# Two transformer blocks on one core: order and banks at the borders of an attention stage changed

## The chip, the cores and the metric

One core of a Trainium2 chip runs the whole program, one launch, everything in fp32. The metric is device time in microseconds (us). A core has a matmul engine (PE, with its weight loads shown apart as PEld), a vector engine (DVE), a scalar engine (ACT), GpSimd (POOL) and a queue engine (SP). Each takes its instructions in the order in which the program lists them and waits on semaphores. PE writes its results into PSUM, eight banks of 128 partitions by 512 fp32 values.

## The reference

256 latent and 256 context tokens of width 1024 run through two layers of a first block, then the latent tokens through two layers of a second. Cut to what matters for the change:

```
first block, each layer:
  mq = rms_norm(rms_norm(c_q, g_qa) @ w_uq)        8 heads of 96: 64 plain, 32 rotated by position
  mk, mv = from rms_norm(c_kv, g_kva) @ w_ukv       mk = rms_norm([k_nope, k_rope], g_mk)
  y_mla  = softmax(mq mk^T / sqrt(96)) mv
  y_na   = softmax over a neighbourhood plus the context keys, with a bias
  x     += gate * merge(sigmoid(g1) * (y_mla @ w_mla_o) + sigmoid(g2) * (y_na @ w_na_o)) @ w_out
  x     += gate * squared_relu(h2 @ w_ff1) @ w_ff2
second block, each layer:
  y = [retention, state space, stick breaking, softmax over a memory], each gated by silu
  x += rms_norm(y @ w_out_2)
```

Layer 0 of the first block computes all 512 tokens, layer 1 needs queries of the 256 latent ones alone; its tiles are half as wide (256 columns).

## The kernel before

Every engine has one program, written out by hand in the order of its work (PE from line 546, ACT from 1314, DVE from 1878). Signals are counted: `signal` lets an instruction raise a semaphore, `event` gives the value on which another engine waits.

*Products.* A product that needs full precision is made of three in a faster format: activation and weight are each split into a high and a low part, and `split_product` (L576 to L580) multiplies high by high, low by high and high by low. The high part of a weight chunk is written by ACT (`split_weights`, L1426 and L1428), the low part by DVE (L1954 and L1957); `split_half` (L1442, L1967) does it in halves between tiles of the attention. The raw chunks come by DMA from SP, each when its slot is free.

*Banks.* `next_bank(key, until=, among=)` calls `take`, which gives the next bank of a ring and lets PE wait until the last user of that bank has signalled its `until`. Each set of banks `among` has a turn counter of its own; calls without `among` go round all eight. The sets in use are the five `TURN_BANKS` for scores and transposes of an attention, bank 5 for its value products, banks 6 and 7 (`GATE_BANKS`) for the gate tiles that fill it, and six `LATE_BANKS` in the second block.

*The way into the attention* (both layers). PE projects keys and plain values: for i from 0 to 9 (L861) a key tile every second step, from step 2 on the sum of squares of head i - 2 (`head_sum`, L659), up to step 7 a value tile. DVE copies the key tile out, ACT squares it, PE sums the squares with ones, ACT takes -0.5 ln and exp (`rms`, L1320 and L1322), DVE scales the key (L2293, L2295). Then come six query tiles (L892, 18 products each): tiles 0 and 3 hold the rotated parts of four heads, the others two heads each. After tiles 1 and 4 PE rotates (`turn_quad`, L665), after tiles 2, 3 and 5 it sums squares (`query_sum`, L889), after tiles 1, 4 and 5 it makes a tile of the latent values (L877). DVE lifts tile 0 or 3 out with its gain (`gain_quad`, L2320), ACT squares it (L1613), DVE applies sine and cosine (L2328 to L2330), adds squares (L2301) and scales the heads (`scale_query`, L2310, L2314); the tiles of two heads stay in their banks until the second head is scaled (`roped`).

*The attention* (`softmax_attention`, L696). Scores run three tiles ahead of transposes: PE score (L925), DVE maximum (L1924), ACT exp (L1397), DVE reciprocal and product (L1928, L1930), PE transpose (L730), ACT copy (L1391), PE value product (L933), DVE copy (L2354). The last two heads' queries are scaled by DVE between the first maxima. From tile 34 (layer 0) or 18 (layer 1) on, PE fills in the eight g1 gate tiles, whose exp ACT takes (`gate_exp1`, L1637).

*The way out.* ACT splits the attention's output (L1647), with the exp of the last g1 tile between its fourth and fifth piece, DVE makes the low parts (L2377). PE runs for n = 0 to 7 the tiles g2, mo, no (24, 12 and 12 products); all three of one n share a weight chunk. In layer 1 DVE makes the low part of the chunk of n = 0 (L1957) after the last copy of the attention.

*The second block* ends each layer with a small attention over a memory (`per` = 2). Behind its last score PE does the first half of output tile 0 (`first_half`, L1214), and then both halves of all eight output tiles (L1206 to L1208), copied out by DVE (L2756).

Of the kernel before, what the change touches and what calls it, by code (L numbers as in the profile page):

```python
# [35 lines left out]
ALU = mybir.AluOpType  # L36
# [3 lines left out]
P = 128  # L40
D, L, T, TC = 1024, 2, 256, 256
KT = D // P
# [14 lines left out]
LINE = 128  # L57
TURN_BANKS, VALUE_BANKS, GATE_BANKS = (0, 1, 2, 3, 4), (5,), (6, 7)
LATE_BANKS = (0, 1, 2, 3, 4, 5)
FILL_FROM, FILL_STEPS = (34, 18), (4, 2)  # L60
GATES = [4, 5, 6, 7, 0, 1, 2, 3] + list(range(8, 16))
ADA = 24
# [201 lines left out]
def program(nc, dram, numbers):  # L264
# [3 lines left out]
    with ctx:  # L268
# [218 lines left out]
        def quad(g):  # L487

            return krope[:, 1 + g, :]
# [57 lines left out]
        def _(pe):  # L547
            used = {"chunk": -1, "open": set()}

            def next_bank(*key, until, among=None):  # L550

                return take(pe, "bank", key, until, among)
# [106 lines left out]
                mm = pe.matmul(ps[0:QK, 0:w], ones[0:QK, 0:QK], s[0:QK, 0:w], start=True, stop=True)  # L659
                full(mm, "ss", (name, i), l)  # L660

            def rotate(key, rows, src, until):

                ps = next_bank(*key, until=until)
                mm = pe.matmul(ps[rows, 0:T], c("rot")[rows, rows], src, start=True, stop=True)  # L665
                full(mm, *key)

# [132 lines left out]
            for l in range(L):  # L800
# [57 lines left out]
                project_heads("nk", 0)  # L858
                pe.wait_ge(*event("kr_gain", l))
                rotate(("krot", l), slice(NOPE, QK), krope[NOPE:QK, 2, TC:TT], ("krot_sin", l))  # L860
                for i in range(NH + 2):  # L861
                    if i < NH and i % 2 == 0:
                        ps = next_bank("mk", l, i // 2, until=("copied", "mk", l, i + 1))
                        mm = linear(ps[:, :], weights("uk", l, i // 2), lambda k: ckv[:, k, :], ("normed", "ckv", l))
                        full(mm, "mk", l, i // 2)
                    if i > 1:
                        head_sum("mk", i - 2, l, TT)

                    if i < NH:
                        nv_tile(l, i // 4, i % 4)  # L870

                def latent_values(t):

                    w = weights("uv", l)
                    ps = next_bank("mv", l, 0, t, until=("v_copied", "mv", l, 0, t))
                    for k in range(2):
                        mm = pe.matmul(ps[:, :], ckv[:, k, P * t:P * t + P], w[:, k, :], start=k == 0, stop=k == 1)  # L877
                    full(mm, "mv", l, 0, t)

                def turn_quad(g):  # L880

                    pe.wait_ge(*event("q_gain", l, g))
                    rotate(("qrot", l, g), slice(0, P), quad(g)[:, TC:TT], ("q_roped", l, g))

                def query_sum(i):

                    ps = next_bank("ss", ("mq", i), l, until=("rs_log", ("mq", i), l))
                    pe.wait_ge(*event("q_added", l, i))
                    mm = pe.matmul(ps[:, 0:cw], pair, given("sq", (("mq", i), l, 0))[:, 0:cw], start=True, stop=True)  # L889
                    full(mm, "ss", ("mq", i), l)  # L890

                for i in range(6):  # L892
                    g, part_of = divmod(i, 3)
                    by = ("q_added", l, 2 * g + 1) if part_of == 0 else ("roped", "mq", l, 4 * g + 2 * part_of - 1)
                    ps = next_bank("mq", l, i, until=by)
                    w = split_weights(("uq", l, i))
                    for k in range(6):
                        if i == 0:
                            pe.wait_ge(*event("cq_lo", l, k))
                        mm = split_product(ps[:, 0:cw], w, k, cq_hi[k][:, t0:TT], cq_lo[:, k, t0:TT], 6)  # L900
                    full(mm, "mq", l, i)
                    if part_of == 1:
                        turn_quad(g)
                    if i in (2, 3, 5):
                        query_sum((0, 0, 0, 1, 0, 2)[i])
                    if i in VALUES_AT:
                        latent_values(VALUES_AT.index(i))
# [123 lines left out]
            for lw in range(L):  # L1031
# [181 lines left out]

                def first_half():  # L1214

                    output_half(next_bank("out2", l, 0, until=("out_copied", l, 0)), 0, 0)

                softmax_attention([(("memory", l), u, 2, mem_score, mem_value) for u in range(8)], 2, mem_gate, first_half)

# [95 lines left out]
        def _(act):  # L1315
# [135 lines left out]
            for l in range(L):  # L1451
# [129 lines left out]
                    projected_keys(lambda: head_rms("nq", 3, t0))  # L1581
                    rms("ckv", l, KVL, P, TT, ("normed", "ckv", l, 1))
                projected_heads("nk", 0)
                for i in range(NH + 2):
                    if i in (0, 2, 3):
                        split_weights(("nv", l, i // 2, i != 2), 1)
                    if i == 0:
                        high_cq(5)
                    if 5 < i < NH:
                        split_weights(("uq", l, i - 6), 1)  # L1590
                    if i < NH:
                        act.wait_ge(*event("copied", "mk", l, i))
                        square(("mk", i), l, 0, 1, mk[0:NOPE, i, :], slice(0, NOPE), kr=i < 4)
                    if i > 1:
                        rms(("mk", i - 2), l, QK, QK, TT, ("k_ready", l, i - 2))
                    if i < NH:
                        j, t = divmod(i, 4)
                        copy_values("nv", l, j, t, nv[:, t, 256 * j:256 * j + 256], ("nv", l, j, t))
# [6 lines left out]
                for i in range(6):  # L1605
                    g, part_of = divmod(i, 3)
                    if i < 4:
                        split_weights(("uq", l, i + 2), 1)
                    act.wait_ge(*(event("psum_full", "mq", l, i) if part_of else event("q_gain", l, g)))
                    ps = bank(("mq", l, i))[:, 0:cw]  # L1610
                    for a in range(2 if part_of == 0 else 0):
                        v = take(act, "sq", ("rope", 2 * g + a, l), ("q_added", l, 2 * g + a))
                        act.activation(v[:, 0:cw], ps, ACT.Square, scale=c("half")[:, a:a + 1]).then_inc(*signal("rope_squared", l, 2 * g + a))  # L1613
                    if part_of:
                        square(("mq", 2 * g + part_of - 1), l, 0, 1, ps)
                    if i in (2, 3, 5):
                        query_rms((0, 0, 0, 1, 0, 2)[i])
                    if i in VALUES_AT:
                        latent_values(VALUES_AT.index(i))
# [19 lines left out]
                softmax([((g[0], l), u, P * g[6]) for g in groups(l) for u in range(2 * NH)], 4, split_gate, ("roped", "mq", l, NH - 1))  # L1639
                for n in range(-(-(16 * len(groups(l)) - FILL_FROM[l]) // FILL_STEPS[l]) - 1, KT - 1):  # L1640
                    gate_exp1(n)
                for k in range(KT):

                    if k == 4:
                        gate_exp1(KT - 1)
                    act.wait_ge(*event("y_copied", ("na", l), NH // 2 - 1))
                    act.activation(b_parts[:, 0, k, t0:TT], y_heads(k)[:, t0:TT], ACT.Copy).then_inc(*signal("b_hi", "y", l, k))  # L1647

# [230 lines left out]
        def _(dve):  # L1879
# [29 lines left out]
                dve.wait_ge(*event(before, *key))  # L1909
                dve.tensor_scalar(e, e, 1.0, 1e19, ALU.add, ALU.min).then_inc(*signal(name, *key))  # L1910

            def softmax(tiles, per, y_out, between=None):

                for i in range(len(tiles) + AHEAD + 3):
                    if i < len(tiles):
# [9 lines left out]
                    if 1 <= i <= len(tiles):  # L1925
                        g, v, w = tiles[i - 1]
                        dve.wait_ge(*event("exp", g, v))
                        then(dve.reciprocal(stat[:, v % 4, 2:3], stat[:, v % 4, 1:2]))  # L1928
                        e = given("prob", (g, v))[:, 0:w]
                        dve.tensor_scalar(e, e, stat[:, v % 4, 2:3], None, ALU.mult).then_inc(*signal("probs", g, v))  # L1930
                    j = i - AHEAD - 3
                    if per == 2 and j >= 0 and j % 2 == 0:
                        y_out(tiles[j][0], tiles[j][1] // 2)
# [127 lines left out]
            for l in range(L):  # L2061
# [213 lines left out]
                then(dve.tensor_tensor(kr, kr, c("cos")[NOPE:QK, :], ALU.mult))  # L2275
                dve.wait_ge(*event("krot_sin", l))
                then(dve.tensor_tensor(kr, kr, e, ALU.add))
                for i in range(NH + 2):
                    if i in (0, 2, 3):
                        split_weights(("nv", l, i // 2, i != 2), 1)  # L2280
                    if i == 0:
# [5 lines left out]
                        dve.wait_ge(*event("psum_full", "mk", l, i // 2))  # L2287
                        dve.tensor_copy(mk[0:NOPE, i, :], bank(("mk", l, i // 2))[r, :]).then_inc(*signal("copied", "mk", l, i))
                    if i > 1:
                        v = i - 2  # L2290
                        dve.wait_ge(*event("rs", ("mk", v), l))
                        r = given("rs", (("mk", v), l))
                        dve.scalar_tensor_tensor(mk[0:NOPE, v, :], mk[0:NOPE, v, :], p("g_mla_k", l)[0:NOPE, :],  # L2293
                                                 r[0:NOPE, :], ALU.mult, ALU.mult)
                        dve.tensor_tensor(mk[NOPE:QK, v, :], krope[NOPE:QK, 2, :], r[NOPE:QK, :], ALU.mult).then_inc(*signal("k_ready", l, v))  # L2295
                def add_rope(i):

                    v = given("sq", (("mq", i), l, 0))[:, 0:cw]
# [33 lines left out]
                for i in range(6):  # L2332
# [2 lines left out]
                        split_weights(("uq", l, i + 2), 1)  # L2335
                    if part_of == 0:
                        gain_quad(g)
                        if g:
                            scale_query(2)
                            scale_query(3)  # L2340
                    else:
# [27 lines left out]
                    for j, a in split_turn(l, i - 1):  # L2369
                        split_half(j, a)  # L2370

                softmax([((g[0], l), u, P * g[6]) for g in groups(l) for u in range(2 * NH)], 4, y_out, with_tile)
                if l:
                    split_weights(("g2", l, 0), 1)
                for k in range(KT):
                    dve.wait_ge(*event("b_hi", "y", l, k))
                    ins = dve.tensor_tensor(b_parts[:, 1, k, t0:TT], y_heads(k)[:, t0:TT],  # L2377
# [525 lines left out]
```

## Time and profile before

| | us |
|---|---|
| median of three runs | 1981.7 (1977.56 to 1983.45) |
| the profiled execution's own time | 1978.23 |
| its span in the trace | 1976.3 |
| PE busy | 1876.7 (95%) |
| DVE busy | 1358.1 (69%) |
| ACT busy | 913.2 (46%) |

The span is what the trace covers; 1.9 us of the execution lie around it. A busy share is a mean over stages. In a row of the timeline the bracket at the end tells how long the engine had been idle before the instruction and whose instruction ended the wait. PE instructions overlap a little, and their ends are modelled, so starts are the safer reading. The ways into the attention lie at 185 to 242 us (layer 0) and 984 to 1020 us (layer 1), the ways out at 366 to 380 and 1094 to 1106 us, the ends of the two memory attentions at 1609 to 1628 and 1906 to 1923 us.

### The profile page before, as it was taken

The numbers are of one execution on the slowest core, as the hardware profiler recorded it, in microseconds if no ns is written. First come the engines' busy times: TensorE is split into PE (matmuls) and PEld (weight loads), VectorE is DVE, ScalarE is ACT, GpSimd is POOL, SyncE is SP. The second block draws the span as 40 slices with busy tenths as digits, with TensorE's granted clock in tenths as the row PEclk, the third lists the DMA queues.
The fourth block names the chain that finished last, engine by engine and source line by source line (L and its number), as shares of the span: only waits on it lengthen the run. The fifth ranks groups of instructions, "written<-read, shape, count | busy, mean of one in ns | idle before, by whom it ended". The sixth has DMA issues, their size and how long they took to land.

```text
span 1976.3 us, 29270 instructions
## 1 busy us (share of the span) xinstructions
PE 1876.7 (95%) x11406; PEld 1590.3 (80%) x11406; DVE 1358.1 (69%) x2421; ACT 913.2 (46%) x1603; POOL 27.8 (1%) x56
## 2 busy tenths in 40 slices
PE   7999999999999999999999989999999989999997
PEld 3777556688888888887756889999999879999886
DVE  6666675688788887765577566665767755767764
ACT  3345565543423231354565654444444643544552
POOL 0000000000000000000000000000000000000000
PEclk9999999999999999999999999999999999999998
DMA  7332201255354545323132454444454325554322
GB/s 290 126 107 68 120 27 60 97 163 183 103 220 176 209 182 202 143 85 101 53 145 68 146 189 169 171 173 157 163 162 138 96 97 171 162 160 141 106 86 97
DMA packets 55896, 272.21 MB, mean 138 GB/s; under 512 B 6352, under 2 KB 7504, under 8 KB 38608
## 3 DMA queue, kind: packets, MB, share of 16 engines
q1 hardware_dynamic: 48272, 225.40, 33.1%
q0 software_dynamic: 7488, 44.94, 6.5%
q8 instruction: 92, 1.51, 0.3%
q14 instruction: 44, 0.36, 0.1%
HBM read 269.27 MB, written 1.05 MB: 137 GB/s over the span
## 4 chain that ended last, share of the span: by engine, by line
PE 71%; DVE 13%; ACT 9%; issue 5%; DMA 1%; SPq 0%; ACTq 0%; DVEq 0%
PE bank L578 18%; PE bank L580 17%; PE bank L579 17%; ACT w_parts L1428 3%; PE bank L925 2%; DVE small_lo L1954 2%; PE bank L933 2%; PE bank L730 2%; PE bank L614 2%; DMA wide<-in_ada 1%; PE bank L1206 1%; PE bank L1208 1%; PE bank L1207 1%; PE bank L625 1%; PE bank L1022 1%
## 5 line engine op out<-in xcount | busy, mean ns | idle before, releaser
L578 PE MATMUL bank<-h_hi,small_hi 128*128 128x256 f32 (+3 forms) x992 | 312.1, 315 | 12.3 <-DVE small_lo L1954 6.2
L579 PE MATMUL bank<-h_lo,small_hi 128*128 128x256 f32 (+3 forms) x992 | 301.8, 304 | 0.0
L580 PE MATMUL bank<-h_hi,small_lo 128*128 128x256 f32 (+3 forms) x992 | 301.7, 304 | 0.0
L1954 DVE TENSOR_TENSOR small_lo<-ring,small_hi 128x1024 fp32r<-128x1024 f32 (+1 forms) x192 | 226.4, 1192 | 107.4 <-ACT small_hi L1426 105.9
L579 PE MATMUL bank<-h_parts,w_parts 128*128 128x256 f32 (+1 forms) x784 | 262.8, 335 | 0.0
L1957 DVE TENSOR_TENSOR w_parts<-ring,w_parts 128x2048 fp32r<-128x2048 f32 x87 | 199.3, 2291 | 91.9 <-ACT w_parts L1428 91.9
L1428 ACT ACTIVATE w_parts<-ring 128x2048 fp32r<-128x2048 f32 x86 | 164.0, 1907 | 176.1 <-PE bank L580 176.1
L578 PE MATMUL bank<-b_parts,w_parts 128*128 128x256 f32 (+1 forms) x656 | 218.8, 334 | 1.5 <-DVE w_parts L1957 1.1
L580 PE MATMUL bank<-b_parts,w_parts 128*128 128x256 f32 (+1 forms) x656 | 217.9, 332 | 0.0
L579 PE MATMUL bank<-b_parts,w_parts 128*128 128x256 f32 (+1 forms) x656 | 217.8, 332 | 0.0
L578 PEld LDWEIGHTS bank<-h_hi,small_hi 128*128 128x128 f32 (+2 forms) x992 | 187.8, 189 | 26.9 <-issue 13.9
L579 PEld LDWEIGHTS bank<-h_lo,small_hi 128*128 128x128 f32 (+2 forms) x992 | 187.8, 189 | 10.9 <-issue 2.2
L1426 ACT ACTIVATE small_hi<-ring 128x1024 fp32r<-128x1024 f32 (+1 forms) x192 | 192.8, 1023 | 6.3 <-DMA ring<-in_w 6.1
L580 PEld LDWEIGHTS bank<-h_hi,small_lo 128*128 128x128 f32 (+2 forms) x992 | 187.6, 189 | 8.8
L578 PE MATMUL bank<-h_parts,w_parts 128*128 128x256 f32 (+1 forms) x528 | 178.4, 338 | 9.8 <-DVE w_parts L1957 4.2
L580 PE MATMUL bank<-h_parts,w_parts 128*128 128x256 f32 (+1 forms) x528 | 176.0, 333 | 0.0
L579 PEld LDWEIGHTS bank<-h_parts,w_parts 128*128 128x128 f32 x784 | 150.2, 192 | 13.5
L578 PEld LDWEIGHTS bank<-b_parts,w_parts 128*128 128x128 f32 x656 | 124.5, 190 | 15.1 <-issue 3.1
L580 PEld LDWEIGHTS bank<-b_parts,w_parts 128*128 128x128 f32 x656 | 124.6, 190 | 12.0
L579 PEld LDWEIGHTS bank<-b_parts,w_parts 128*128 128x128 f32 x656 | 124.6, 190 | 11.9
L578 PEld LDWEIGHTS bank<-h_parts,w_parts 128*128 128x128 f32 x528 | 101.2, 192 | 21.9 <-issue 9.3
L2010 DVE SCALAR_TENSOR_TENSOR prob<-lowrank,c_rows 128x1024 f32<-128x1024 f32 x96 | 113.3, 1217 | 0.0
(300 smaller groups left out, 3759.0 us busy)
## 6 DMA issues: line engine op xcount, KB each, us to landing
ring<-in_w SPq DMA_DIRECT2D x204, 512.0 KB, 3.5
ring<-in_w SPq DMA_DIRECT2D x96, 1024.0 KB, 4.8
lowrank<-in_rows POOLq DMA_DIRECT2D x24, 1024.0 KB, 5.1
prob<-in_rows POOLq DMA_DIRECT2D x24, 512.0 KB, 3.8
wide<-in_ada SPq DMA_DIRECT2D x8, 1024.0 KB, 9.9
ring<-in_w SPq DMA_DIRECT2D x14, 384.0 KB, 3.1
lowrank<-in_bias POOLq DMA_DIRECT2D x2, 2048.0 KB, 11.2
x<-in_x SPq DMA_DIRECT2D x2, 1024.0 KB, 9.9
```

Source lines behind the costliest of these rows:

```text
L578: pe.matmul(ps, w[0][:, k, :], hi, start=k == 0, stop=False)
L579: pe.matmul(ps, w[0][:, k, :], lo, start=False, stop=False)
L580: return pe.matmul(ps, w[1][:, k, :], hi, start=False, stop=k == nk - 1)
L614: mm = pe.matmul(out, w[:, k, :], src(k), start=first and k == 0, stop=last and k == nk - 1)
L730: mm = pe.transpose(ps[:, P * k:P * k + P], given("prob", (g, u))[:, P * k:P * k + P], ident)
L925: return pe.matmul(ps[:, 0:P * nk], qs[r, a, q:q + P], ks[r, a, 0:P * nk], start=True, stop=True)
L933: mm = pe.matmul(ps[VD * a:VD * a + VD, 0:T], vs[:, k, v:v + VD], turned[:, a, k, :], start=k == 0, stop=k == nk - 1)
L1426: act.activation(small_hi[:, pair, 0:size], small[:, slot, 0:size], ACT.Copy).then_inc(*signal("w_hi", i))
L1428: act.activation(w_parts[pair][:, 0, 0:size], ring[:, slot, 0:size], ACT.Copy).then_inc(*signal("w_hi", i))
L1954: dve.tensor_tensor(small_lo[:, slot, 0:size], small[:, slot, 0:size], small_hi[:, pair, 0:size].bitcast(F32), ALU.subtract).then_inc(*sig ...
L1957: dve.tensor_tensor(w_parts[pair][:, 1, 0:size], ring[:, slot, 0:size], w_parts[pair][:, 0, 0:size].bitcast(F32), ALU.subtract).then_inc(* ...
L2010: ins = dve.scalar_tensor_tensor((product1 if l else product if b < 40 else product2)[:, s, :], w, 1.0, c_rows[:, s, :], ALU.mult, ALU.mul ...
```

## The change

- The square sum of the last key head moves from before query tile 0 to after it on PE; its logarithm and exp (ACT) and its scaling (DVE) move behind the work on query tile 0.
- Query tiles 1 to 5 take banks 0, 3, 5, 6, 7; rotations and square sums of queries take turns in banks 1 and 4; latent value tiles take bank 2, the last of them bank 5. All of these took turns in all eight before.
- The exp of the last g1 tile moves ahead of the splitting of the attention's output.
- In layer 1 the low part of chunk n = 0 moves ahead of the last copies of the attention's output.
- The first half of output tile 0 takes a bank of `GATE_BANKS`.

```diff
+QUERY_BANKS, LATENT_BANKS, QUERY_TILES = (1, 4), (2,), (None, (0,), (3,), (5,), (6,), (7,))
 # PE
-            def rotate(key, rows, src, until):
+            def rotate(key, rows, src, until, among=None):
-                ps = next_bank(*key, until=until)
+                ps = next_bank(*key, until=until, among=among)
...
-                for i in range(NH + 2):
+                for i in range(NH + 1):
...
-                    ps = next_bank("mv", l, 0, t, until=("v_copied", "mv", l, 0, t))
+                    ps = next_bank("mv", l, 0, t, until=("v_copied", "mv", l, 0, t), among=VALUE_BANKS if t == 3 else LATENT_BANKS)
-                    rotate(("qrot", l, g), slice(0, P), quad(g)[:, TC:TT], ("q_roped", l, g))
+                    rotate(("qrot", l, g), slice(0, P), quad(g)[:, TC:TT], ("q_roped", l, g), QUERY_BANKS)
-                    ps = next_bank("ss", ("mq", i), l, until=("rs_log", ("mq", i), l))
+                    ps = next_bank("ss", ("mq", i), l, until=("rs_log", ("mq", i), l), among=QUERY_BANKS)
-                    ps = next_bank("mq", l, i, until=by)
+                    ps = next_bank("mq", l, i, until=by, among=QUERY_TILES[i])
                     full(mm, "mq", l, i)
+                    if i == 0:
+                        head_sum("mk", NH - 1, l, TT)
...
-                    output_half(next_bank("out2", l, 0, until=("out_copied", l, 0)), 0, 0)
+                    output_half(next_bank("out2", l, 0, until=("out_copied", l, 0), among=GATE_BANKS), 0, 0)
 # ACT
-                for i in range(NH + 2):
+                for i in range(NH + 1):
...
+                    if i == 0:
+                        key_rms(NH - 1)
                     if i in (2, 3, 5):
                         query_rms((0, 0, 0, 1, 0, 2)[i])
...
+                gate_exp1(KT - 1)
                 for k in range(KT):
-                    if k == 4:
-                        gate_exp1(KT - 1)
                     act.wait_ge(*event("y_copied", ("na", l), NH // 2 - 1))
 # DVE
+                    if beyond and i == len(tiles):
+                        beyond()
                     j = i - AHEAD - 3
...
-                for i in range(NH + 2):
+                for i in range(NH + 1):
...
                         gain_quad(g)
-                        if g:
+                        if g == 0:
+                            scale_key(NH - 1)
+                        else:
                             scale_query(2)
                             scale_query(3)
...
-                softmax([((g[0], l), u, P * g[6]) for g in groups(l) for u in range(2 * NH)], 4, y_out, with_tile)
-                if l:
-                    split_weights(("g2", l, 0), 1)
+                softmax([((g[0], l), u, P * g[6]) for g in groups(l) for u in range(2 * NH)], 4, y_out, with_tile,
+                        (lambda: split_weights(("g2", l, 0), 1)) if l else None)
```

`key_rms(i)` is the old `rms(("mk", i), ...)` and `scale_key(v)` the old pair of DVE instructions, each as a function.

## Rows read from the trace of the kernel before

**Rows 1.** Windows: stretch, us, busy PE, PEld, DVE, ACT, POOL, PEclk, DMA
```profile
374.00:520.00 146.00, 143.90 (x705) 122.11 (x704) 115.12 (x186) 65.53 (x92) 8.47 (x16) 0.99 0.43 144
520.00:700.00 180.00, 177.33 (x786) 146.88 (x786) 150.27 (x221) 54.21 (x53) 10.57 (x20) 0.99 0.54 194
```
**Rows 2.** Waits of PE, whole span: us in total, times, longest
```profile
PE bank L578 <- DVE w_parts L1957: 10.6, 13, 2.8
```
**Rows 3.** Timeline of PE, layer 0, last key sum and query tile 1: start, us
```profile
189.08 1.14 PE L659 MATMUL bank<-sq,con 96*96 96x512 f32 x1 [2.34 <-ACT sq L1334]
...
195.66 0.39 PE L578 MATMUL bank<-cq_hi,small_hi 128*128 128x512 f32 x1
```
**Rows 4.** Windows behind three waits of PE
```profile
189.10:192.15 3.05, 3.05 (x6) 1.68 (x6) 1.87 (x3) 2.99 (x6) 0.00 (x0) 0.50 0.06 24
...
373.70:376.40 2.70, 2.70 (x6) 2.16 (x7) 2.64 (x5) 2.70 (x5) 0.00 (x0) 0.50 0.00 0
...
1101.05:1103.90 2.85, 2.85 (x24) 2.85 (x25) 2.85 (x9) 2.33 (x3) 0.00 (x0) 1.00 0.66 201
```
**Rows 5.** Timeline of PE, layer 0, scores 2 and 3 and transpose 4
```profile
232.82 3.41 PE L925 MATMUL bank<-wide 96*128 96x512 f32 x4 [3.57 <-DVE wide L2314]
...
241.78 0.63 PE L730 MATMUL bank<-con,prob 128*128 128x128 f32 x4
```
**Rows 6.** Timeline of DVE, layer 0, maximum of score 2
```profile
234.56 0.69 DVE L1924 TENSOR_REDUCE stat<-bank 128x1 f32<-128x512 f32 x1 [1.79 <-PE bank L925]
```
**Rows 7.** Timeline of ACT, layer 0, exp of score 5
```profile
240.85 0.69 ACT L1397 ACTIVATE prob<-bank,stat 128x512 f32<-128x512 f32 x1
```
**Rows 8.** Timeline of PE, layer 0, last value product and first g2 tile
```profile
368.52 1.95 PE L933 MATMUL bank<-probT,wide 128*64 128x256 f32 x16 [0.73 <-issue]
373.69 0.80 PE L578 MATMUL bank<-h_hi,w_parts 128*128 128x512 f32 x1 [3.22 <-ACT wide L1637]
```
**Rows 9.** Timeline of PE, layer 1, key sum 6, rotation 0, query sum 0
```profile
984.77 1.02 PE L659 MATMUL bank<-sq,con 96*96 96x512 f32 x2
...
993.61 0.70 PE L665 MATMUL bank<-prob,con 128*128 128x256 f32 x2 [1.73 <-DVE prob L2320]
...
998.02 0.60 PE L889 MATMUL bank<-sq,con 128*128 128x256 f32 x2
```
**Rows 10.** Timeline of DVE, layer 1, scaling of key 7 and gain of tile 0
```profile
990.61 0.75 DVE L2293 SCALAR_TENSOR_TENSOR wide<-wide,par,rs 64x512 f32<-64x512 f32 x1
...
993.07 0.48 DVE L2320 TENSOR_SCALAR prob<-bank,gq 128x256 f32<-128x256 f32 x1
```
**Rows 11.** Timeline of ACT, layer 1, logarithm for key 7, squares of tile 0
```profile
989.01 0.67 ACT L1320 ACTIVATE rs<-bank,con 96x512 f32<-96x512 f32 x1
...
993.59 0.84 ACT L1613 ACTIVATE sq<-bank,con 128x256 f32<-128x256 f32 x2 [2.52 <-DVE prob L2320]
```
**Rows 12.** Timeline of PE, layer 1, first g2 tile
```profile
1101.05 0.36 PE L578 MATMUL bank<-h_hi,w_parts 128*128 128x256 f32 x1 [2.81 <-DVE w_parts L1957]
```
**Rows 13.** Timeline of ACT, layer 1, high parts of chunks 2 and 3
```profile
1107.56 1.90 ACT L1428 ACTIVATE w_parts<-ring 128x2048 fp32r<-128x2048 f32 x1
...
1114.09 1.90 ACT L1428 ACTIVATE w_parts<-ring 128x2048 fp32r<-128x2048 f32 x1
```
**Rows 14.** Timeline of DVE, layer 1, low part of chunk 1
```profile
1103.51 2.29 DVE L1957 TENSOR_TENSOR w_parts<-ring,w_parts 128x2048 fp32r<-128x2048 f32 x1
```
**Rows 15.** Timeline of DVE, second block, layer 0, first stick-breaking logits
```profile
1567.16 0.56 DVE L2662 TENSOR_SCALAR probT<-bank 128x384 f32<-128x384 f32 x1 [0.48 <-PE bank L1038]
```
**Rows 16.** Timeline of PE, second block, start of first half output tile, both layers
```profile
1615.23 0.39 PE L1206 MATMUL bank<-y_hi,small_hi 128*128 128x256 f32 x1 [1.62 <-DVE wide L2734]
...
1910.27 0.47 PE L1206 MATMUL bank<-y_hi,small_hi 128*128 128x256 f32 x1
```
**Rows 17.** Timeline of PE, second block, layer 1, start of output tile 1
```profile
1920.41 0.36 PE L1206 MATMUL bank<-y_hi,small_hi 128*128 128x256 f32 x1 [0.41 <-DVE small_lo L1954]
```
**Rows 18.** Timeline of DVE, second block, layer 1, copy of output tile 0
```profile
1921.31 0.42 DVE L2756 COPY probT<-bank 128x256 f32<-128x256 f32 x1
```

More of the change, by code:

```diff
@@ L1583, in _, with key_rms @@
                 projected_heads("nk", 0)
-                for i in range(NH + 2):
+                def key_rms(i):
+                    rms(("mk", i), l, QK, QK, TT, ("k_ready", l, i))
+                for i in range(NH + 1):
                     if i in (0, 2, 3):
@@ L1594, in _ @@
                     if i > 1:
-                        rms(("mk", i - 2), l, QK, QK, TT, ("k_ready", l, i - 2))
+                        key_rms(i - 2)
                     if i < NH:
@@ L1910, in one_plus, with softmax @@
                 dve.tensor_scalar(e, e, 1.0, 1e19, ALU.add, ALU.min).then_inc(*signal(name, *key))
-            def softmax(tiles, per, y_out, between=None):
+            def softmax(tiles, per, y_out, between=None, beyond=None):
                 for i in range(len(tiles) + AHEAD + 3):
@@ L2277, in _, with scale_key @@
                 then(dve.tensor_tensor(kr, kr, e, ALU.add))
-                for i in range(NH + 2):
+                def scale_key(v):
+                    dve.wait_ge(*event("rs", ("mk", v), l))
+                    r = given("rs", (("mk", v), l))
+                    dve.scalar_tensor_tensor(mk[0:NOPE, v, :], mk[0:NOPE, v, :], p("g_mla_k", l)[0:NOPE, :],
+                                             r[0:NOPE, :], ALU.mult, ALU.mult)
+                    dve.tensor_tensor(mk[NOPE:QK, v, :], krope[NOPE:QK, 2, :], r[NOPE:QK, :], ALU.mult).then_inc(*signal("k_ready", l, v))
+                for i in range(NH + 1):
                     if i in (0, 2, 3):
@@ L2289, in _ @@
                     if i > 1:
[L2290 to L2295, printed above, removed]
+                        scale_key(i - 2)
                 def add_rope(i):
```

## The prediction

> **What bounds the kernel now.** I read the windows by stage first: between 374 and 700 us PE is busy 143.9 of 146 and 177.3 of 180 us [rows 1]. What PE gains ahead of such a stretch reaches the end, and the change matters only where PE stands still. So next the waits of PE, then the timeline around each border. Three kinds of wait lie there. PE waits for a chain (the square of the last key, 2.34 us [rows 3]; the gain of query tile 0, 1.73 us [rows 9]). PE waits for a bank whose old user is late: scores 2 and 3 stand 3.57 us behind L2314, the scaling of the very last head [rows 5], which they don't read; query tile 5 held their bank. The first g2 tile stands 3.22 us behind the exp of the last g1 tile [rows 8], again a bank, and the first half output tile of the second block's layer 0 stands 1.62 us [rows 16] behind a gated product. Or PE waits for a low weight part (2.81 us [rows 12], part of 10.6 us in 13 waits [rows 2]).
>
> The waits cost more than their length where the clock falls. Behind the 2.34 us wait PE ran 3.05 us at a granted clock of 0.50 (1.2 GHz), behind the 3.22 us wait 2.70 us, behind the 2.81 us wait none, at 1.00 (2.4 GHz) [rows 4]. Half such a stretch is lost: 1.5 and 1.35 us.
>
> **The change part by part**, against the profiled execution.
>
> *Last key sum behind query tile 0, layer 0.* PE goes straight on. Removed: 2.34 us and 1.5 us of clock. Behind tile 0 the square is long made. Rotation 0 comes some 4 us earlier and needs the gain of tile 0; DVE has the 1.5 us of key 7 moved behind it, so it is ready just before. The first query sum then has nearly no slack (DVE now scales key 7 ahead of it), but it holds. **-3.9.**
>
> *Query banks, layer 0.* Scores 2 and 3 no longer wait for L2314. DVE still scales the last head first, until 232.8, and takes the maximum of score 2 there instead of at 234.56 [rows 6]: 1.8 us earlier. From there a tile costs DVE 1.35 us, ACT must take exp 5 behind a weight half, and transpose 4 (at 241.78 [rows 5]) takes the bank of score 5, so it waits for that exp (240.85 [rows 7]), which moves to about 238.3. PE could gain 3.4, the DVE and ACT queues let 2.5 through. Bounds 1.8 and 3.6. **-2.5.**
>
> *Way out, layer 0.* The g2 tile now stands in a bank that a transpose left, and the exp of g1 is early too. PE goes on at 368.52 + 1.95 = 370.5 instead of 373.69 [rows 8], and the 1.35 us of clock go: 4.6. What is late next? The split output is needed 5.6 us later by mo and is ready by then (the splitting itself loses the exp from its middle); chunk 1 too. **-4.6.** These three, 11.0, cross a stretch that PE bounds [rows 1].
>
> *Way in, layer 1.* Here the sum turns, and the place is a bank. Before, the ring of all eight stands alike in both layers: key sum 6 in bank 5. The change takes 15 calls out of the ring per layer (five query tiles, two rotations, four sums, four value tiles), and 15 is one short of 16, so in layer 1 the ring stands one bank on: key sum 6 in bank 6, query tile 0 in bank 7, key sum 7 in bank 0. Query tile 1 is fixed to bank 0. It must wait until ACT has taken the logarithm of key sum 7, and that is now queued behind the squares of tile 0, which need DVE's gain, which stands behind the scaling of key 6. In numbers: key sum 6 starts at 984.77 [rows 9]; a sum is 1.0, a tile of 18 products 18 x 0.119 = 2.1 (24 took 2.85 [rows 4]), so tile 0 and key sum 7 end at 988.9. On DVE key 7's 1.5 us leave the place in front of the gain: the weight part starts at 990.6 where they started, the gain (0.48) at 991.6 [rows 10]. ACT: two squares 0.8, the logarithm 0.7 [rows 11], done at 993.6. PE stands still for 4.7 us, then has tile 1 (2.1) and the 4.4 us that lie between rotation 0 and query sum 0 (993.61 to 998.02 [rows 9]): sum 0 at 1000.1, 2.1 late. Behind a wait of this length I expect the low clock, 2.7 to 3.05 us of it [rows 4], 1.4 more. Everything behind hangs on sum 0 through the chain ln, exp, scale, gain, so nothing is won back. Bounds 2.1 and 5. **+3.5.**
>
> In sentences of its own: the Trainium skill, page "TensorE: Matmul & The Clock Gate", section on the HAM clock gate, says that how many matmuls run at the low rate differs from run to run of the same kernel. Two of three waits here paid it [rows 4]. Without any clock term the sum below would be 1.4 us less gain here, 2.9 less in layer 0, so -7.2 in place of -8.7.
>
> *Query banks, layer 1.* Transpose 0 no longer waits for the last head, but ACT, with exp 2 ahead, takes it no sooner. Bounds 0 and 1. **-0.1.**
>
> *Way out, layer 1.* The first g2 tile starts 2.81 us sooner [rows 12]. But this stage isn't bound by PE: ACT's high parts come every 1114.09 - 1107.56 = 6.5 us [rows 13], where 48 products take 5.7. ACT splits a chunk, DVE makes the low part and the gate's 1 + e, ACT takes its ln and exp before it splits again. PE's lead is lost in waits for L1957, and the end moves by what the loop's start moves: DVE took chunk 1 at 1103.51 [rows 14], behind eight low parts held up by exp (0.3) and the chunk 0 part; now at 1103.1. Bounds 0 and 2.8. **-0.4.**
>
> *Second block.* The ring stands two on in its first layer. The first stick-breaking score then follows the product of gate tile 10, not 11; DVE stood 0.48 us there [rows 15]. **-0.5**, bounds 0 and 2.2. The half output tile loses its wait, as in the other layer, where none stands before it [rows 16]: **-1.6**, and the chain behind it starts with its transposes. In the last layer the half tile had no wait to lose. There it takes gate bank 7 and the ring then gives bank 7 to output tile 1, which must wait until DVE has copied tile 0: 1921.31 + 0.42, about 1921.8, where tile 1 started at 1920.41 [rows 17, 18]. PE bounds from there to the end. Bounds 0 and 1.5. **+1.4.**
>
> Sum: -3.9 - 2.5 - 4.6 + 3.5 - 0.1 - 0.4 - 0.5 - 1.6 + 1.4 = **-8.7**. Its own 1978.2 becomes 1969.5. The median of the runs shown lies 3.5 above that execution, so as a median 1981.7 - 8.7 = **1973.0**.
>
> **The rivals.**
>
> *A. The bank of tile 1 in layer 1 is free in time* (my count of the ring is off by one, or the logarithm comes sooner). Then rotation 0 follows the gain at 992.1, and query sum 0 meets DVE's adds, which key 7 has pushed back, at about 998.2: +0.2 for +3.5, so -12.0, 1969.7. For it: one call miscounted does it. Against: both layers stood alike before.
>
> *B. Layer 0's gain leaks away.* The key sum's slack on DVE is nil: if key 7's scaling (1.5 us) delays the first query sum by 1.5, and the row and weight work of DVE (150 of 180 us [rows 1]) swallows half of 11.0, the sum is -8.7 + 1.5 + 5.5 = -1.7, 1980.0. Against: PE shows only 2.7 us idle in those 180.
>
> *C. Slower.* The long wait in layer 1 doesn't cost 3 us of low clock but leaves PE at 1.2 GHz through the whole way in, from 993.6 to 1020 and on into the attention, whose short waits keep it there. Each us of PE's work costs another one; work of 18 us more at the low rate would give back the gain of 8.7 and 9 more, +9, 1990.7. It decides from 9 us on. For it: in the attention's first tiles PE has small gaps. Against: behind both waits of layer 0 the clock rose within 3.05 us [rows 4].
>
> *D. The borders don't bind* (waits move to the next instruction, all within 0.3%): the three largest waits turn into others, -3, 1978.7. For it: PE, DVE and ACT form a ring of waits at the way in, and of its 3.4 us I already count only 2.5.
>
> **How the numbers follow.** Forecast 0.62, A 0.12, B 0.10, D 0.11, C 0.05. The forecast's own range is -5 to -12 (the clock terms, and the bounds of layer 1): 1969.5 to 1976.5. With A below and B and D above, and the spread of the runs shown (5.9 us between three), the range is 1965.5 to 1979.5. About 0.3%, 5.9 us, is what a measurement of this kernel can tell from no change: the limit is 1975.8. Faster: most of the forecast (0.54 of 0.62), A, a little of B: 0.70. Slower: C: 0.05. Same: 0.25.
>
> **What would show it.** Right: in layer 0 no wait before the last key sum, scores 2 and 3 or the first g2 tile, and g2 some 10 to 11 us earlier; in layer 1 a wait of 4 to 5 us of PE before query tile 1, ended by ACT's L1320 line, with a granted clock near 0.50 behind it; a first g2 tile without a wait for L1957 and then more waits for it in the same loop; in the last layer a wait of 1.5 to 2 us before output tile 1, ended by the copy. Wrong: no wait at query tile 1 in layer 1 (A); waits of PE for L2301 in layer 0 (B); a clock of 0.5 for longer than 4 us (C).

## The result, and the profile after

The changed kernel takes 1971.27 us (median of 4, 1969.78 to 1972.47), the kernel before 1982.26 us in the same session: ratio 0.9945, interval 0.9927 to 0.9963, so 11.0 us faster (7.3 to 14.5). The forecast was 1973.0. The profiled execution has a span of 1967.8 us against 1976.3: 8.5 us less, where the sum said 8.7.

I read the change by PE's lead: the start of one instruction before, less its start after. Row by row it shows where the time went. PE's timeline of the changed kernel (start, us; the line numbers stand up to 12 higher than before), layer 0: last key sum and query tile 1, rotation 0, last query sum, scores 1 to 3, transpose 4, last value product, first g2 tile.

```profile
190.01 1.02 PE L660 MATMUL bank<-sq,con 96*96 96x512 f32 x2
190.47 0.80 PE L579 MATMUL bank<-cq_hi,small_hi 128*128 128x512 f32 x1
...
194.98 0.59 PE L666 MATMUL bank<-prob,con 128*128 128x256 f32 x2
...
220.03 1.02 PE L890 MATMUL bank<-sq,con 128*128 128x512 f32 x2
...
223.47 2.74 PE L928 MATMUL bank<-wide 96*128 96x512 f32 x6
...
234.36 0.63 PE L731 MATMUL bank<-con,prob 128*128 128x128 f32 x4 [0.57 <-ACT prob L1400]
...
361.12 1.95 PE L936 MATMUL bank<-probT,wide 128*64 128x256 f32 x16 [0.73 <-issue]
363.00 0.50 PE L579 MATMUL bank<-h_hi,w_parts 128*128 128x512 f32 x1
```

No bracket stands at the key sum, the scores or the g2 tile: the waits of [rows 3], [rows 5] and [rows 8] are gone. Transpose 4 now waits for ACT's exp, as forecast. The kernel before had rotation 0 here:

```profile
199.74 0.59 PE L665 MATMUL bank<-prob,con 128*128 128x256 f32 x2
```

The lead there is 199.74 - 194.98 = 4.76 us (by chance the length of a wait in layer 1, below). Then layer 1 and the second block: query tile 1, rotation 0, query sum 0, the first g2 tile and the g2 tile of n = 1; then the first half output tile of the second block's layer 0 (1602.16) and output tile 1 of its layer 1 (1910.48).

```profile
979.75 0.46 PE L579 MATMUL bank<-cq_hi,small_hi 128*128 128x256 f32 x1 [4.76 <-ACT rs L1323]
...
983.51 0.60 PE L666 MATMUL bank<-prob,con 128*128 128x256 f32 x2
...
987.82 0.59 PE L890 MATMUL bank<-sq,con 128*128 128x256 f32 x2
...
1087.97 0.39 PE L579 MATMUL bank<-h_hi,w_parts 128*128 128x256 f32 x1
...
1095.38 0.36 PE L579 MATMUL bank<-h_hi,w_parts 128*128 128x256 f32 x1 [1.40 <-DVE w_parts L1965]
...
1602.16 0.47 PE L1209 MATMUL bank<-y_hi,small_hi 128*128 128x256 f32 x1
...
1910.48 0.39 PE L1209 MATMUL bank<-y_hi,small_hi 128*128 128x256 f32 x1 [1.78 <-DVE probT L2768]
```

The forecast waits stand at their places: 4.76 us before query tile 1, for the logarithm L1323 (L1320 before); a g2 tile without a wait and a wait for the low part one tile later; 1.78 us before output tile 1, for the copy. The lead at each place, and what each step gave:

| stretch | lead at its end | gave | forecast |
|---|---|---|---|
| up to key sum 6, layer 0 | 0.66 | -0.66 | 0 |
| key sum behind tile 0 (rotation 0) | 4.76 | -4.10 | -3.9 |
| scores, layer 0 (transpose 4) | 7.42 | -2.66 | -2.5 |
| way out, layer 0 | 12.06 | -4.64 | -4.6 |
| 503 to 960 us, nothing changed | 13.83 | -1.77 | 0 |
| way in, layer 1 (query sum 0) | 10.20 | +3.63 | +3.5 |
| attention, layer 1 | 10.20 | 0.00 | -0.1 |
| way out, layer 1 (1167.30) | 10.57 | -0.37 | -0.4 |
| stick breaking, second block | 11.10 | -0.53 | -0.5 |
| first half output tile | 13.07 | -1.97 | -1.6 |
| behind a 2.32 us wait, not changed | 11.50 | +1.57 | 0 |
| stretch before output tile 0, last layer | 11.30 | +0.20 | 0 |
| output tile 1, last layer | 9.93 | +1.37 | +1.4 |
| behind that wait | 8.40 | +1.53 | 0 |

What the forecast doesn't have is the clock. Windows of the changed kernel (stretch, us, then busy PE, PEld, DVE, ACT, POOL, then PEclk, DMA share and GB/s) behind four waits of 4.76, 2.67, 2.32 and 1.78 us:

```profile
979.75:983.15 3.40, 3.40 (x16) 3.40 (x17) 2.39 (x3) 1.34 (x2) 0.00 (x0) 0.52 0.00 0
513.80:517.20 3.40, 3.40 (x15) 2.81 (x16) 3.40 (x7) 1.31 (x3) 0.38 (x1) 1.00 0.73 236
1614.20:1617.60 3.40, 3.39 (x18) 3.40 (x19) 1.97 (x3) 2.04 (x3) 0.00 (x0) 0.59 0.15 60
1910.50:1913.90 3.40, 3.40 (x20) 3.40 (x21) 2.04 (x2) 2.28 (x3) 0.00 (x0) 0.68 0.30 123
```

And the kernel before, behind the same wait as the second row (there at 525.86 us):

```profile
525.90:529.30 3.40, 3.40 (x10) 2.68 (x11) 3.40 (x7) 1.33 (x3) 0.41 (x1) 0.63 0.72 243
```

The wait is the same 2.67 us in both and the change is far from it, but only the kernel before paid behind it: 10 products in the window instead of 15. That is the -1.77. Two unchanged waits, one on each side of it, show the lead before and after (the kernel before, then the changed one):

```profile
516.73 0.39 PE L578 MATMUL bank<-h_parts,w_parts 128*128 128x256 f32 x1 [1.17 <-DVE h_parts L2440]
...
893.24 1.10 PE L625 MATMUL bank<-sq,con 128*128 128x256 f32 x4 [2.23 <-DVE sq L1900]
```

```profile
504.65 0.38 PE L579 MATMUL bank<-h_parts,w_parts 128*128 128x256 f32 x1 [1.18 <-DVE h_parts L2452]
...
879.41 0.89 PE L626 MATMUL bank<-sq,con 128*128 128x256 f32 x3 [2.24 <-DVE sq L1906]
```

Behind the 2.32 us wait it is the other way round: only the changed kernel paid there.

### The profile page after: what moved, and what is told of

Read it like the earlier page. It is cut to its first block, busy times and chain, and to the rows that moved or that the text cites. A ratio compares the mean times of both kernels' runs of the same rounds, so it can differ in the third digit from the quotient of the medians.

```text
span 1967.8 us, 29270 instructions
## 1 busy us (share of the span) xinstructions
PE 1874.7 (95%) x11406; PEld 1590.6 (81%) x11406; DVE 1357.8 (69%) x2421; ACT 913.0 (46%) x1603; POOL 27.8 (1%) x56
## 4 chain that ended last, share of the span: by engine, by line
PE 73%; DVE 12%; ACT 8%; issue 5%; DMA 2%; SPq 0%; ACTq 0%; DVEq 0%
PE bank L579 18%; PE bank L581 17%; PE bank L580 17%; ACT w_parts L1431 3%; DVE small_lo L1962 2%; PE bank L928 2%; PE bank L936 2%; PE bank L615 2%; PE bank L731 2%; PE bank L1209 2%; PE bank L1210 2%; PE bank L1211 2%; DMA wide<-in_ada 1%; PE bank L626 1%; PE bank L1025 1%
```

## The experiments

All ratios are to the kernel before, which ran in the same rounds.

**The two new waits.** `a1_swap`: 0.9933 (0.9922 to 0.9945). `a2_out_ring`: 0.9932 (0.9919 to 0.9946). `a3_both`: 0.9920 (0.9907 to 0.9933). The changed kernel itself, run beside them (`a4_again`), had 0.9950 (0.9938 to 0.9961).

```diff
+QUERY_TILES_1 = (None, (3,), (0,), (5,), (6,), (7,))                # a1, a3
-ps = next_bank("mq", l, i, until=by, among=QUERY_TILES[i])
+ps = next_bank("mq", l, i, until=by, among=(QUERY_TILES_1 if l else QUERY_TILES)[i])
-... next_bank("out2", l, 0, until=("out_copied", l, 0), among=GATE_BANKS) ...   # a2, a3
+... next_bank("out2", l, 0, until=("out_copied", l, 0), among=None if lw else GATE_BANKS) ...
```

> The changed kernel, but in layer 1 query tiles 1 and 2 exchange banks: tile 1 takes bank 3, tile 2 bank 0. Theory (the bank of key sum 7 holds query tile 1): the 4.76 us wait of PE before tile 1 of layer 1 goes, with the 1.7 us of low clock behind it; rotation 0 then waits for the gain of tile 0, query sum 0 comes some 3.5 us earlier against the stage's start, and the time falls by 2.5 to 3.5 us against the changed kernel (ratio to the kernel before 0.9930). Rival (the chain of the queries through ACT and DVE sets query sum 0, because the work on key 7 was moved into it): the wait moves to rotation 0 and query sum 0, under 1 us is won, ratio 0.9942.

> The changed kernel, but in the last layer the first half output tile takes its bank from the ring of all eight, as before the change; in the layer ahead of it the gate bank stays. Theory (output tile 1 waits for tile 0's copy because both get bank 7): the 1.78 us wait before output tile 1 shrinks to the 0.4 us of before, the time falls by 1.4 us, by 2.9 if the 1.5 us of low clock that stood behind the wait go too. Rival (the wait is only put off, to output tile 2 or 3): 0, the end of the last layer comes at the same distance from its first output tile.

> Both edits of the two kernels ahead together. If the two waits are independent the gains add: 4 to 6 us under the changed kernel, ratio to the kernel before 0.9920. If PE's lead is taken by something later, less than the larger of the two.

PE's timeline of `a1_swap`, rotation 0 and query sum 0 of layer 1:

```profile
981.43 0.70 PE L667 MATMUL bank<-prob,con 128*128 128x256 f32 x2 [1.16 <-DVE prob L2332]
...
987.55 0.67 PE L891 MATMUL bank<-sq,con 128*128 128x256 f32 x2 [1.56 <-DVE sq L2313]
```

The bank was the cause: no wait stands before tile 1. The way in now costs 0.22 us more than before the change (the +0.2 of rival A), against +3.63: 1.7 of the 3.4 saved is clock, the other 1.7 wait. The queries' chain holds what is left in two waits. In `a2_out_ring` output tile 1 waits as in [rows 17]:

```profile
1910.84 0.35 PE L1209 MATMUL bank<-y_hi,small_hi 128*128 128x256 f32 x1 [0.41 <-DVE small_lo L1962]
```

1.4 us of wait and 1.5 us of low clock behind it are gone, 2.9 us in all. Together the ratios fall by 0.0030, 6 us, as two independent waits should; the single steps of 3.4 us lie inside the intervals, the traces carry them.

**The same programs once more.** No edit.

> The changed kernel once more, for a second profile. Theory (which wait is followed by a low clock differs from execution to execution of one program): starts of PE agree to 0.1 us within each stage, but at least one of the low-clock stretches of the first profile (at 36, 978, 1170, 1614, 1872, 1911 us) is missing or a new one appears, each worth 1.0 to 1.8 us. Rival (the program alone decides): the same stretches, the same span to 0.3 us. Ratio to the kernel before 0.9945 either way.

> The kernel before once more, for a second profile. Theory (a wait of PE of 2 us or more is followed by a low clock in some executions and not in others, so the kernel with more such waits loses more on average): the starts of PE agree with the first profile stage by stage, but more low-clock stretches show than the 20.9 us of lost clock of the first profile, in particular behind the 2.81 us wait of layer 1's first g2 tile or the 2.24 us wait at 1566 us, which had none; span 1978 to 1983. Rival (the first profile is typical, and the 3.5 us between it and the median are something else): lost clock 20 to 22 us and a span near 1976 in spite of a time ratio of 1.000.

`a4_again`: 0.9950 (0.9938 to 0.9961), span 1971.9 us. `d1_before_again`: 1.0007 (0.9998 to 1.0015), span 1982.2 us. The changed kernel's second profile, behind the wait of 2.67 us, which ends at 515.06, and the one before query tile 1:

```profile
515.06:518.46 3.40, 3.40 (x8) 2.76 (x9) 3.40 (x7) 1.28 (x3) 0.36 (x1) 0.51 0.68 236
984.60:991.40 6.80, 6.80 (x29) 5.58 (x29) 3.90 (x7) 1.52 (x4) 0.00 (x0) 0.65 0.20 58
```

The first wait is followed by 0.51 where the first profile has 1.00. At the second the low clock lasts twice as long, 6.8 us: it begins 1.5 us before the wait ends (at 984.11), so 5.3 us of it lie behind, and 2.7 us are lost there instead of 1.7. I added up the lost clock of a whole profile (half of each low stretch, leaving out what lies in waits of PE over 0.1 us, and the last 13 us, where PE has nothing left to do): before 12.8 and 20.2 us, after 11.1 and 15.4. Taken off the spans that leaves 1963.5 and 1962.0 before, 1956.7 and 1956.6 after. So two executions of one program differ by 4 and 6 us in span, and by 0.1 and 1.5 us once the clock is taken off; on the means, the change is worth 6.1 us at full clock, and 3.3 us more because it leaves fewer long waits. (Low clock in a stretch that PE doesn't bound costs nothing, so such a sum is an upper bound. With two profiles of each, the 3.3 are a mean of two.)

**Which edit did the way out of layer 0?**

```diff
 # b1_exp_back, in the changed kernel; b2_exp_only is the reverse, in the kernel before
-                gate_exp1(KT - 1)
                 for k in range(KT):
+                    if k == 4:
+                        gate_exp1(KT - 1)
```

> The changed kernel, but the exp of the last g1 tile stands again between the fourth and fifth piece of ACT's splitting, in both layers. Theory (the 3.22 us wait of the first g2 tile in layer 0 was a bank's alone, and the change has moved that tile to a bank which a transpose left): no wait before the first g2 tile, the time within 0.5 us of the changed kernel (ratio 0.9945 to 0.9950). Rival (the move of the exp took the wait away): the wait of about 3.2 us is back with its low clock, 3 to 5 us slower than the changed kernel, ratio 0.997.

> The kernel before, with nothing changed but the exp of the last g1 tile moved ahead of the splitting. The first g2 tile of layer 0 still has the bank of the last g1 tile. Theory (either of the two edits is enough, since the exp then runs at about 368.3 us, before the last value products end): the 3.22 us wait goes, and what the clock behind it cost (1.4 to 1.7 us, where it fell), so -3.2 to -4.9 us, ratio 0.9978. Rival (the bank must go): the wait keeps more than 2 us, ratio 0.9995.

`b1_exp_back`: 0.9950 (0.9939 to 0.9962). `b2_exp_only`: 0.9967 (0.9955 to 0.9979). The first g2 tile of each:

```profile
364.21 0.50 PE L579 MATMUL bank<-h_hi,w_parts 128*128 128x512 f32 x1
```

```profile
372.24 0.50 PE L578 MATMUL bank<-h_hi,w_parts 128*128 128x512 f32 x1
```

Neither has a wait. The exp alone removes it, the bank alone removes it: the two edits are one gain twice over. The lead of `b2_exp_only` grows by 4.66 us across it, 3.22 of wait and the rest clock. Its time fell by 6.5 us (4.2 to 8.9), more than the 4.9 that I gave as the most; the lower part of the interval agrees.

**The order alone.** The change without its banks and without its ways out:

```diff
-                    ps = next_bank("mq", l, i, until=by, among=QUERY_TILES[i])
+                    ps = next_bank("mq", l, i, until=by)
... and so for qrot, ss of mq, mv and out2; gate_exp1 and the low part of g2 as before
```

> The kernel before, with the last key sum alone moved behind query tile 0 (with its logarithm, exp and scaling), all banks in the ring of eight. Theory: in layer 0 the 2.34 us wait goes, with the clock 4.1 us; the 3.57 us wait of scores 2 and 3 stays; in layer 1 no wait before query tile 1, but waits for the gain (about 1.2) and for the adds (about 1.5), query sum 0 at +0.2 us. Sum -3.9, ratio 0.9980. Rival (the reorder and the banks help only together, since PE would wait for a bank behind the moved sum): waits of over 1 us for a bank in layer 0, ratio 1.000.

0.9975 (0.9966 to 0.9984). Score 2 and the first g2 tile:

```profile
229.06 2.93 PE L928 MATMUL bank<-wide 96*128 96x512 f32 x3 [3.57 <-DVE wide L2326]
...
371.12 0.59 PE L579 MATMUL bank<-h_hi,w_parts 128*128 128x512 f32 x1 [3.22 <-ACT wide L1645]
```

Both bank waits stand as they did, layer 0's key sum has none, and layer 1's way in costs 0.24 us, with the waits of 1.18 and 1.56 us that `a1_swap` has too. The reorder doesn't need the banks. 5.0 us (3.2 to 6.7) hold the 3.9 expected.

**The bank of query tile 5.**

```diff
+QUERY_TILES_0 = (None, (0,), (7,), (5,), (6,), (2,))
+... among=(QUERY_TILES if l else QUERY_TILES_0)[i])
-... among=VALUE_BANKS if t == 3 else LATENT_BANKS)
+... among=VALUE_BANKS if t == 3 else LATENT_BANKS if l else (3,))
```

> The changed kernel, but in layer 0 query tile 5 takes bank 2, one of the five that the attention's scores turn in (query tile 2 takes bank 7, latent values bank 3): score 2 takes bank 2 again. Theory (a bank alone made scores 2 and 3 wait for the scaling of the last head): the wait before score 2, ended by DVE's scaling of the last head, is back with about 3.5 us, and transpose 4 comes 1.5 to 2.7 us later than in the changed kernel, counted from the last query sum; ratio to the kernel before 0.9955. Rival (DVE's order holds the stage anyway: it takes the maximum of score 2 only behind the last head): the wait is back, but transpose 4 moves by less than 1 us, ratio 0.9948.

0.9976 (0.9966 to 0.9985). Score 2 and transpose 4:

```profile
228.27 2.08 PE L929 MATMUL bank<-wide 96*128 96x512 f32 x2 [3.57 <-DVE wide L2326]
...
238.12 0.63 PE L732 MATMUL bank<-con,prob 128*128 128x128 f32 x4
```

The wait is back to the hundredth. Transpose 4 comes 17.87 us behind the last query sum (220.25), against 14.33 in the changed kernel: 3.5 us, more than I gave. The granted clock from 227.5 to 234.5 us is 0.57, 3 us lost, 2.6 of them behind the wait, where the kernel before lost 1.7 behind the same wait [rows 5]; 0.9 of the 3.5 are this, which leaves 2.6 for the bank. With the longer low stretch PE was late for transpose 4, and the row has no wait for the exp any more. The ratio was forecast as 0.9955. By the ratios the time is 5 us above the changed kernel's, 3.5 of them here; the rest I can't place.

**The low part of layer 1.**

```diff
-                softmax(..., with_tile, (lambda: split_weights(("g2", l, 0), 1)) if l else None)
+                softmax(..., with_tile)
+                if l:
+                    split_weights(("g2", l, 0), 1)
```

> The changed kernel, but in layer 1 the low part of chunk 0 stands again behind the last copies of the attention. Theory (the way out of layer 1 is bound by the splitting of weights on ACT and DVE, not by PE's start): the first g2 tile waits 2.8 us again, the waits for low parts later in the loop shrink, the output loop ends within 0.6 us of where the changed kernel's ends (counted from the last value product); ratio 0.9945 to 0.9950. Rival (the move is worth its wait): 2.8 us slower, ratio 0.9960.

0.9949 (0.9938 to 0.9961). The wait stands again:

```profile
1094.87 0.36 PE L579 MATMUL bank<-h_hi,w_parts 128*128 128x256 f32 x1 [2.81 <-DVE w_parts L1965]
```

Against the changed kernel it is 4.02 us late before the loop and 4.37 behind it: of 2.81 us of wait 0.35 count. The loop is bound by ACT and DVE, as [rows 13] had it.

**Further on.** With both repairs, the scaling of key 7 behind the adds of query sum 0; then also the gains for the next memory, one behind each output copy:

```diff
                         gain_quad(g)
-                        if g == 0:
-                            scale_key(NH - 1)
...
                         add_rope(2 * g + part_of - 1)
+                        if i == 1:
+                            scale_key(NH - 1)
 # d5_gain_spread also
-                if lw + 1 < L:
-                    ... for k in range(KT): memory_gain(l + 1, k)
                 for n in range(KT):
                     ...
+                    if lw + 1 < L:
+                        memory_gain(l + 1, n)
```

> The changed kernel with both bank repairs (query tiles 1 and 2 exchange banks in layer 1, the last layer's first output tile takes a ring bank), and the scaling of key 7 on DVE moved from behind the gain of tile 0 to behind the adds of query sum 0. Theory (the scaling of key 7, which waits 2.13 us for ACT, pushed rotation and adds back): the 1.56 us wait of PE before query sum 0 of layer 1 goes, 1.5 us under the kernel with both repairs, ratio to the kernel before 0.9912; layer 0 unchanged, as PE didn't wait there. Rival (ACT is the bound, its logarithm and exp of key 7 stand ahead of the squares that the adds need): the wait keeps over 1 us, ratio 0.9920.

> The kernel with the late scaling of key 7, and in the second block's first layer the eight gains of the next memory (2.19 us of DVE ahead of the first output copies) spread one behind each output copy. Theory (they hold up the low part that output tile 0's second half or tile 1 waits 2.32 us for): that wait goes and with it the 1.7 us of low clock that stood behind it in every profile of the changed kernel: -2.3 to -4.0 us, ratio 0.9895. Rival (the wait is for the high part on ACT or the weight's arrival): under 0.5 us, ratio 0.9910.

`d4_key_late`: 0.9933 (0.9920 to 0.9946), nothing won. The wait before query sum 0 is 0.82 us in place of 1.56, and one of 0.37 is new before the second rotation, with the key's scaling now ahead of it: from key sum 6 to the last query sum it takes 26.3 us, as in `a3_both`. The ratio (0.9912 was forecast) lies above that of `a3_both`, 0.9920, at the edge of its interval, in another session. The work has to stand somewhere in DVE's queue. `d5_gain_spread`: 0.9909 (0.9896 to 0.9922), 1964.13 us (median of 5), the lowest ratio of all, though the interval overlaps that of `a3_both`. The ratio is what the rival named (0.9910), but only because the kernel it builds on came out at 0.9933; the trace decides for the theory. Output tile 1 of the second block's first layer:

```profile
1614.42 0.36 PE L1210 MATMUL bank<-y_hi,small_hi 128*128 128x256 f32 x1 [0.41 <-DVE small_lo L1963]
```

2.32 us of wait became 0.41, and the low clock behind it is gone: PE gains 3.4 us on `d4_key_late` there, and keeps them.

Not tried: the query banks without the reorder. In layer 1, by my count of the ring, tiles 0 and 1 would then both have bank 0, and the adds that free tile 0's bank wait for tile 2. And the first half output tile in the ring in the second block's first layer: by my count it would hold bank 4, which transpose 6 takes before it can be copied. So its gate bank isn't only a gain, the other edits need it.

## Why the prediction was right

*The key sum* was sized at -3.9 and gave -4.10; the feared loss at query sum 0 didn't come (rival B out: no wait of PE for the adds stands in layer 0).

*The query banks* were sized -2.5 and gave -2.66. Bank 2 back brings the 3.57 us back. That the gain stops short of the wait because transpose 4 then waits for exp 5 is in the row at 234.36.

*The way out of layer 0*: -4.6, gave -4.64. The reason given named both edits; each alone is enough.

*The way in of layer 1*: +3.5, gave +3.63, by the bank that the ring's 15 missing calls moved. Shown by `a1_swap`. The count of a ring decided this term; the profile before had no row for it.

*The way out of layer 1*: -0.4, gave -0.37, the 2.8 us lost again in the loop. *The second block*: the first half tile was sized -1.6 from the wait alone and gave -1.97; the shared bank at the end +1.4 and gave +1.37 as a wait; with the clock behind it that bank cost 2.9 us, twice the term.

*The clock* is the term that was mis-sized. I added it at three waits and left it out at the others. Where I added it, its size was near: 1.35 for the first g2 tile, where 1.4 stood behind the wait, and 1.4 before query tile 1 of layer 1, where it was 1.7 (2.7 in `a4_again`). Where I left it out, it came: behind the 1.78 us wait at output tile 1 in four of six profiles. And it came or stayed away behind waits that the change doesn't touch, -1.77 and +1.57 between these two executions. That 8.5 met 8.7 owes something to luck: the steps that were forecast, as measured, sum to -9.3, and what the forecast had at 0 (-0.66, -1.77, +1.57, +0.20, +1.53) to +0.9. The kernel before's profiled execution (1978.23) lies 4.0 us under its median, the changed one's (1969.78) 1.5 under; I had carried 3.5 over to both, and so 8.7 stands against 11.0. In `d1_before_again` the 2.81 us wait of layer 1 paid, which [rows 4] show at 1.00. The Trainium skill, page "TensorE: Matmul & The Clock Gate", section on the HAM clock gate, says of a kernel's start that the number of matmuls at the low rate varies between runs of one kernel; these profiles show the same in mid-kernel (8 and 15 products in the 3.4 us behind the same 2.67 us wait). Without any clock term my sum stood at -7.2; at full clock the spans differ by 6.1. Rival C's mechanism, a clock that stays at 1.2 GHz through the whole way in, didn't show in six profiles; the longest stretch was some 7 us. One slip of arithmetic: -5 to -12 from 1981.7 is 1969.7 to 1976.7, not 1969.5 to 1976.5.

What stays open is about 1.6 us of the 11.0, as the mean spans of two profiles each differ by 9.4; that is well inside the interval, and `a4_again` with 0.9950 gives 9.9.

## What to carry to other kernels

Where banks go round a ring, write out who takes which bank in every pass, before and after: taking 15 calls out of a ring of eight made a collision in layer 1 that the kernel before had in neither layer. It cost 3.6 us beside a gain of 11, and exchanging two banks gave 3.4 back. Two edits with one wait between them count once: take each alone before adding them up. And add the clock behind each long wait of PE as a chance, not as a row of one profile.

## What the runs showed of the hardware

The granted clock behind one and the same wait of PE, over 14 profiles of this kernel's versions. "Low" means a stretch at 0.5 (1.2 GHz) of 3.4 us (short) or 6.8 us (long), which begins between 2.0 us before the wait's end and 2.0 us behind it; otherwise the clock is 1.00 (2.4 GHz):

| wait of PE | low in |
|---|---|
| 4.76 us, query tile 1, layer 1 | 6 of 6 (2 short, 4 long) |
| 3.57 us, score 2, layer 0 | 5 of 5 (1 short, 4 long) |
| 3.22 us, first g2 tile, layer 0 | 3 of 3 |
| 2.81 us, first g2 tile, layer 1 | 3 of 5 |
| 2.75 us, product near 1171 us | 14 of 14 |
| 2.67 us, weight's low part near 514 us | 11 of 14 |
| 2.59 us, product near 38 us | 13 of 14 |
| 2.34 us, last key sum, layer 0 | 3 of 3 |
| 2.32 us, output tile 1, second block's first layer | 11 of 13 |
| 2.24 us, square sum near 880 us | 7 of 14 |
| 2.24 us, second block, near 1566 us | 2 of 4 |
| 1.99 us, square sum near 1873 us | 14 of 14 (all long) |
| 1.78 us, output tile 1, last layer | 4 of 6 |
| 1.73 us, rotation 0, layer 1 | 0 of 3 |
| 1.41 us, transpose, layer 0, near 229 us | 2 of 9 |

The length of the wait alone doesn't settle it: the 1.99 us wait was followed by a long low stretch every time, the 2.24 us wait near 880 us in half of the profiles. What one low stretch costs is half of what lies behind the wait: 1.4 to 1.7 us for a short one where PE sets the pace, up to 3.4 for a long one. Why a stretch comes in one execution and not in another stays open.

The times of one program spread by up to 8 us (before: 1977.1 to 1985.0), while between such stretches PE's starts keep their distances to 0.1 us. A difference of 1.7 us between two profiles is no finding until the clock behind each wait has been compared.
